# State-space stage: outputs on two column halves, lag products on four column quarters, preparation reordered

## What is computed

```python
h = rmsnorm(x, norm_mix[i])
a_bar = jnp.exp(lam * dt)
b_bar = ((a_bar - 1.0) / lam)[..., None] * lax.complex(b_re, b_im)
bu = jnp.einsum('blgh,gph->blgp', ug, b_bar)
_, states = lax.associative_scan(_ssm_combine, (a_seq, bu), axis=1)
y = jnp.einsum('blgp,ghp->blgh', states, c).real.reshape(bsz, length, D_MODEL)
y = jax.nn.gelu(y + d_skip * u)
val, gate = jnp.split(y @ w_glu, 2, axis=-1)
return val * jax.nn.sigmoid(gate)
```

## Time and profile before

| | us |
|---|---|
| median of 3 runs | 1874.41 (1874.4 to 1874.81) |
| the profiled execution, its own time | 1875.26 |
| its span, first to last instruction | 1873.5 |
| PE busy in the span | 1832.2 |
| end of the changed stage (first GLU product) | 144.8 |

### The profile page before, as it was taken

The page is one execution under the profiler, slowest core; times in us unless marked ns, Lnnn a source line. Parts: engine busy times, 40 slices in busy tenths (PEclk is TensorE's granted clock), DMA queues, the critical chain, the costliest instruction groups (busy, mean ns, idle before and its releaser), DMA issues.

```text
span 1873.5 us, 23935 instructions
## 1 busy us (share of the span) xinstructions
PE 1832.2 (98%) x9343; PEld 1476.4 (79%) x9343; DVE 1164.0 (62%) x1690; ACT 839.9 (45%) x1340; POOL 748.9 (40%) x429
## 2 busy tenths in 40 slices
PE   6999999999999999999999999999999999999998
PEld 5888888888887778668888888887776868888886
DVE  8974234735566588872356365641636658887978
ACT  6743343333335445683333233353457464343444
POOL 1214344343434368543443434334346454334322
PEclk9999999999999999999999999999999999999999
DMA  6424443052321222103532424125110223325041
GB/s 167 103 39 158 124 154 94 27 176 68 113 68 41 94 75 91 46 2 113 157 90 67 146 58 129 51 82 152 57 68 22 81 90 113 119 62 162 19 135 45
DMA packets 199979, 171.24 MB, mean 91 GB/s; under 512 B 19002, under 2 KB 174090, under 8 KB 199802
## 3 DMA queue, kind: packets, MB, share of 16 engines
q1 hardware_dynamic: 197554, 165.93, 29.5%
q10 hardware_dynamic: 2312, 3.78, 0.6%
HBM read 162.58 MB, written 2.65 MB: 88 GB/s over the span
## 4 chain that ended last, share of the span: by engine, by line
PE 88%; ACT 4%; DVE 4%; issue 1%; DMA 1%; POOL 1%; SPq 0%; POOLq 0%; DVEq 0%; ACTq 0%
PE PS L2644 75%; PE PS L3006 2%; PE PS L2997 2%; PE PS L3016 2%; DMA xp<-in_x 1%; PE PS L2542 1%; PE PS L2543 1%; PE PS L2563 1%; PE PS L2575 1%; DVE taken L2374 1%; PE PS L2956 1%; PE PS L2923 0%; ACT probs_t L1457 0%; PE PS L2584 0%; PE PS L2590 0%
## 5 line engine op out<-in xcount | busy, mean ns | idle before, releaser
L781 POOL TENSOR_TENSOR w_lo<-raw,w_hi 128x2048 fp32r<-128x2048 f32 x92 | 430.2, 4676 | 609.8 <-ACT w_hi L1074 608.4
L2644 PE MATMUL PS<-xT_hi,w_hi 128*128 128x512 f32 (+1 forms) x1160 | 444.4, 383 | 3.1 <-DVE xT_lo L1903 2.0
L2644 PE MATMUL PS<-xT_lo,w_hi 128*128 128x512 f32 (+1 forms) x1160 | 441.6, 381 | 0.0
L2644 PE MATMUL PS<-xT_hi,w_lo 128*128 128x512 f32 (+1 forms) x1160 | 441.4, 380 | 0.0
L1074 ACT ACTIVATE w_hi<-raw 128x2048 fp32r<-128x2048 f32 x105 | 201.2, 1916 | 332.0 <-PE PS L2644 332.0
L2644 PEld LDWEIGHTS PS<-xT_hi,w_hi 128*128 128x128 f32 x1160 | 217.8, 188 | 50.1 <-issue 8.6
L2644 PEld LDWEIGHTS PS<-xT_lo,w_hi 128*128 128x128 f32 x1160 | 217.8, 188 | 42.2
L2644 PEld LDWEIGHTS PS<-xT_hi,w_lo 128*128 128x128 f32 x1160 | 217.9, 188 | 41.1
L788 POOL TENSOR_TENSOR w_lo<-dn_raw,w_hi 128x1024 fp32r<-128x1024 f32 (+1 forms) x52 | 138.5, 2685 | 249.5 <-ACT w_hi L1225 249.5
L2644 PE MATMUL PS<-w_hi,xT_hi 128*128 128x512 f32 (+1 forms) x560 | 220.0, 393 | 1.0 <-issue 1.0
L2644 PE MATMUL PS<-w_hi,xT_lo 128*128 128x512 f32 (+1 forms) x560 | 216.6, 387 | 0.0
(11 more groups left out here) (425 smaller groups left out, 2843.2 us busy)
## 6 DMA issues: line engine op xcount, KB each, us to landing
raw<-in_ffn_w_gate_up SPq DMA_DIRECT2D x88, 512.0 KB, 5.1
dn_raw<-in_ffn_w_down SPq DMA_DIRECT2D x22, 1024.0 KB, 7.8
raw<-in_w_up SPq DMA_DIRECT2D x32, 512.0 KB, 5.4
dn_raw<-in_w_down SPq DMA_DIRECT2D x16, 1024.0 KB, 7.9
raw<-in_dsa_w_in SPq DMA_DIRECT2D x28, 512.0 KB, 4.4
raw<-in_w_in SPq DMA_DIRECT2D x21, 512.0 KB, 4.8
raw<-in_s_w_glu SPq DMA_DIRECT2D x16, 512.0 KB, 4.5
raw<-in_dsa_w_o SPq DMA_DIRECT2D x8, 512.0 KB, 4.5
```

What stands on the lines that cost most here:

```text
L781: pool.tensor_tensor(w_lo[:, g % 2, :], raw[:, r % 2, :], f32(w_hi[:, g % 2, :]), ALU.subtract).then_inc(w_split, 1)
L2644: ins = mm(o, a if weights_stay else c, c if weights_stay else a, start=first and n == 0, stop=last and n == 2, skip_group_check=onto)
```

## The change

1. **Outputs on two column halves.** `s5_out` is split. `s5_out_taps(b)` makes the eight taps products, `s5_out(b)` sixteen state products (the output map's two products, which DVE used to subtract, are now added by PE in PSUM). Groups 0 to 3 of a block go to PSUM rows 0 to 63 and groups 4 to 7 to rows 64 to 127, in turns. Gelu handles 128x512 instead of 64x1024, the `y` layout changes, and the turns on the way out are 32 transposes of 128x128. The GLU weights are loaded in the matching row order: four DMAs for a slot where there were two.
2. **Lags on four quarters.** The 8 groups go to PSUM rows 0, 32, 64 and 96, two each: 8 products of 16 columns, 16 of 112, and 4 for the skip term. `lag_out` becomes four instructions of 16x256. The lags have two PSUM banks in turns, so PE no longer waits for the last copy.
3. **Output map.** Two unlinked DVE products of 128x1024 (signs moved into the ACT copies of C), no difference.
4. **Preparation.** The powers take four linked instructions a step where there were six. ACT scales rows 0 and 4, makes table 0, then rows 1 to 3; DVE scales rows 5 to 7. PE turns five row sets ahead of the loop and three in its first pass; the second half of the value product and of `kv_done` moves behind the first `s5_in`.
5. **Tables.** Parts 1 to 3 are made by ACT in passes 0 to 2 of the block loop, behind the copies of the pass and ahead of its gelu; SP issues the copy of part b+1 behind the taps of block b.
6. **Order.** PE: rotate in, input, lags, turn of the input map, rotate out, output taps, output. ACT: lag copy first, then states.

```diff
@@ constants
-TURN_BANKS = [4, 5, 6, 0, 1, 2, 3, 7]
+U_BY_ACT, U_BY_DVE = (0, 4, 1, 2, 3), (5, 6, 7)
+TURN_BANKS, U_EARLY = [5, 1, 6, 2, 3, 0, 7, 6], 5
@@ SyncE
+                for b in range(2):
+                    for t in range(2):
+                        cols = slice(D * t + 256 * j, D * t + 256 * j + 256)
+                        put(raw_of(g) % 2, v[GP * b:GP * b + GP, :, t, :], glu[b][:, k:k + 4, cols])
...
                             for s in range(CH):
                                 sp.dma_start(tp[GH * s:GH * s + GH, :, s:CH, :].rearrange("p g t h -> p g (t h)"),
                                              lag[:, :, 0:CH - s, :].rearrange("p g t h -> p g (t h)")).then_inc(s5_taps, 16)
+                            if b < TABS - 1:
+                                table_copy(b + 1)
                             if b == 0:
-                                table_copy(1)
                                 sp.wait_ge(kv_sb, 2)
                                 sp.dma_start(kv_dram, kv_new[:, :, :]).then_inc(kv_out, 16)
-                                table_copy(2)
                             if b == 1:
-                                table_copy(3)
                                 glu_load(0, 0, 0)
@@ ScalarE
-            for s in range(CH):
+            for s in U_BY_ACT:
                 act.wait_ge(s5_rstd, 1 + s // (CH // 2))
-                if s == CH // 2:
-                    kv_copy(0)
                 act.activation(u[:, :, s, :], xp[:, s, :].rearrange("p (g h) -> p g h", h=GH), ACT.Copy,
                                scale=rstd[0:NC, s:s + 1]).then_inc(s5_u, 1)
+                if s == 4:
+                    act.wait_ge(s5_u, 2)
+                    table(0)
...
+                for q in range(4):
+                    ins = act.activation(lag[:, 2 * q:2 * q + 2, :, :].rearrange("p g t h -> p (g t h)"),
+                                         PS[32 * q:32 * q + GH, b % 2, 0:2 * P], ACT.Copy)
+                ins.then_inc(s5_lag_sb, 1)
...
             in_map_out(0)
+            kv_copy(0)
+            turned_rows(0, U_EARLY)
             lag_out(0)
-            table(0)
+            decay_out(0)
             kv_copy(1)
...
-            table(1)
-            table(2)
             for b in range(NB - 1):
+                lag_out(b + 1)
+                if b == 0:
+                    turned_rows(U_EARLY, NB)
                 states_out(b)
-                lag_out(b + 1)
                 decay_out(b + 1)
                 if b + 2 < NB:
                     in_map_out(b + 2)
-                if b == 0:
-                    table(3)
+                if b < TABS - 1:
+                    table(b + 1)
                 gelu(b)
@@ VectorE
-                link(tt(o[:, :, :, :], over_k(c_n, b, CH + 1), p_re, ALU.mult))
-                link(tt(tmp_a[:, :, :, :], over_k(c_s, b, CH + 1), p_im, ALU.mult))
-                tt(o[:, :, :, :], o[:, :, :, :], tmp_a[:, :, :, :], ALU.subtract).then_inc(s5_outa, 1)
+                tt(out_re[b % 3][:, :, :, :], over_k(c_n, b, CH), p_re, ALU.mult)
+                tt(out_im[b % 3][:, :, :, :], over_k(c_s, b, CH), p_im, ALU.mult).then_inc(s5_outa, 1)
...
+            dve.wait_ge(s5_rstd, 2)
+            for s in U_BY_DVE:
+                ts(u[:, :, s, :], xp[:, s, :].rearrange("p (g h) -> p g h", h=GH), rstd[0:NC, s:s + 1], None, ALU.mult).then_inc(s5_u_dve, 1)
...
-                    dve.wait_ge(x_hi_done, j0 + n_th + 1)
+                    dve.wait_ge(x_hi_done, j0 + n_th + (2 - n_th % 2 if view else 1))
@@ TensorE
+            def s5_out_taps(b):
+                pe.wait_ge(s5_taps, 16 * CH * (b + 1))
...
+                for g in range(GB // 2):
+                    for side in range(2):
+                        at = GB // 2 * side + g
+                        mm(s5_out_at(b, side, g), uT[:, GB * b + at, :], tp[:, at, :, :].rearrange("p t h -> p (t h)"), start=g == 0, stop=False)
...
+                for j in range(2):
+                    for q in range(4):
+                        g = GB * b + 2 * q + j
+                        mm(at(q, j)[:, 0:GH], b_n[:, g, :], c_n[:, g, :], start=j == 0, stop=False)
...
             for b in range(NB - 1):
                 s5_rotate_in(b)
                 s5_in(b + 1)
                 s5_lags(b + 1)
-                s5_rotate_out(b)
+                if b == 0:
+                    pe.wait_ge(s5_lag_sb, 1)
+                    pe.wait_ge(kv_sb, 2)
+                    u_turn(U_EARLY, NB)
                 if b + 2 < NB:
                     s5_in_turn(b + 2)
-                else:
+                s5_rotate_out(b)
+                if b == 0:
+                    pe.wait_ge(s5_ut_sb, NB)
+                s5_out_taps(b)
+                if b + 2 == NB:
                     s5_rotate_in(b + 1)
                 s5_out(b)
+            s5_out_taps(NB - 1)
             pe.wait_ge(s5_lag_sb, NB)
             s5_rotate_out(NB - 1)
-            s5_turn(0, 4)
+            s5_turn(0, 2)
             s5_out(NB - 1)
-            s5_turn(4, NB)
+            s5_turn(2, 4)
```

More of the change, by code:

```diff
@@ L256, in program @@
         small = place("small", "arena", 82 * KB, [P, 18, G])
[L257 to L260, removed]
+        pw = place("pw", "spare", 0, [P, 2, G, CH + 1])
+        pw_r, pw_i = pw[:, 0, :, :], pw[:, 1, :, :]
+        pw_is = place("pw_is", "spare", 4608, [P, G, CH + 1])
         uT = place("uT", "x_hi", 0, [P, G, NC])
@@ L1056, in states_out @@
                 act.activation(states[:, :, :].rearrange("p g c -> p (g c)"), PS[:, 5, :], ACT.Copy).then_inc(s5_x_sb, 1)
[L1058 to L1067, removed]
             def round_slot(g):
                 r = raw_of(g)
-                act.wait_ge(w_raw[r % 2], (r // 2 + 1) * 32)
+                act.wait_ge(w_raw[r % 2], 32 * (r // 2 + 1) + 32 * min(r // 2 + 1, GLU_SLOTS // 2))
                 if g >= 2:
@@ L1074, in round_slot, with turned_rows @@
                 act.activation(w_hi[:, g % 2, :], raw[:, r % 2, :], ACT.Copy).then_inc(w_rounded, 1)
+            def turned_rows(first, last):
+                for q in range(first, last):
+                    act.wait_ge(s5_ut, q + 1)
+                    act.activation(uT[:, GB * q:GB * q + GB, :].rearrange("p g c -> p (g c)"), PS[:, TURN_BANKS[q], :], ACT.Copy).then_inc(s5_ut_sb, 1)
             in_map_out(0)
+            kv_copy(0)
+            turned_rows(0, U_EARLY)
             lag_out(0)
-            table(0)
+            decay_out(0)
             kv_copy(1)
-            for q in range(8):
-                act.wait_ge(s5_ut, q + 1)
-                act.activation(uT[:, GB * q:GB * q + GB, :].rearrange("p g c -> p (g c)"), PS[:, TURN_BANKS[q], :], ACT.Copy).then_inc(s5_ut_sb, 1)
-            decay_out(0)
             in_map_out(1)
-            table(1)
-            table(2)
             for b in range(NB - 1):
+                lag_out(b + 1)
+                if b == 0:
+                    turned_rows(U_EARLY, NB)
                 states_out(b)
-                lag_out(b + 1)
                 decay_out(b + 1)
@@ L2522, in _, with kv_values @@
             ins.then_inc(kv_done, 1)
-            def kv_values(m):
-                for k in range(KT):
+            def kv_values(m, first=0, last=KT):
+                for k in range(first, last):
                     ins = mm(PS[:, 7, MEM * m:MEM * m + MEM], memT[:, k, P * m:P * m + P], w_kv[:, 1, k, :], start=k == 0, stop=k == KT - 1)
@@ L2532, in _, with s5_out_at @@
             kv_values(0)
+            def s5_out_at(b, side, g):
+                return PS[GP * side:GP * side + GP, 6 + b % 2, P * g:P * g + P]
+            def s5_out_taps(b):
+                pe.wait_ge(s5_taps, 16 * CH * (b + 1))
+                tp = taps[(b + 1) % 2]
+                if b >= 2:
+                    pe.wait_ge(s5_gelu, b - 1)
+                for g in range(GB // 2):
+                    for side in range(2):
+                        at = GB // 2 * side + g
+                        mm(s5_out_at(b, side, g), uT[:, GB * b + at, :], tp[:, at, :, :].rearrange("p t h -> p (t h)"), start=g == 0, stop=False)
             def s5_out(b):
                 pe.wait_ge(s5_x_sb, b + 1)
-                pe.wait_ge(s5_taps, 16 * CH * (b + 1))
-                tp = taps[(b + 1) % 2]
-                if b >= 1:
-                    pe.wait_ge(s5_gelu, b)
-                for g in range(GB):
-                    o = PS[0:NC, 6 + g // 4, P * (g % 4):P * (g % 4) + P]
-                    mm(o, uT[:, GB * b + g, :], tp[:, g, :, :].rearrange("p t h -> p (t h)"), start=True, stop=False)
-                    ins = mm(o, states[:, g, :], out_a[b % 3][:, g, 1:CH + 1, :].rearrange("p t h -> p (t h)"), start=False, stop=True)
+                for g in range(GB // 2):
+                    for m in (out_re, out_im):
+                        for side in range(2):
+                            at = GB // 2 * side + g
+                            ins = mm(s5_out_at(b, side, g), states[:, at, :], m[b % 3][:, at, :, :].rearrange("p t h -> p (t h)"),
```

(1 more changed line is left out.)

156 lines of the change are left out of this document (81 added, 75 removed).

## The result

The changed kernel took 1907.44 us (median of 4 runs, 1906.39 to 1909.1), the kernel before 1874.61 (1874.4 to 1875.08) beside it: ratio 1.0174, 95% interval 1.0162 to 1.0186, so 32.8 us slower. The forecast was 1895.9 with 1887 to 1904: the direction and the mechanism were right, the size was 11.5 us short and the time lies outside the range. The profiled execution had 1906.39 (span 1904.6), 31.1 us of span more than the one before.

The account below looks back on a forecast made before the run. PE was taken as the bound, 88% of the chain. Preparation, three table passes, quicker blocks and way out summed to +20.8 us at the GLU start; with 0.8 for low clock +21.5, forecast 1895.9 us, range 1887 to 1904.

Parts of the forecast that it names:

- a low clock behind the start: At the GLU's start: PE idle before it, so one 6.8 us low-clock stretch, half behind the start; 0.8 us at even odds.
- What PE and DVE gain: Block loop: overlapping column halves and quarters cut PE's block from 10.43 to 8.75 us and DVE's to 8.5.
- The ring: Block loop: table copies ahead of the next taps put tables into the lag-copy cycle; three passes 49.8 us, before 31.3.
- The passes: Passes 0, 1 and 2 of the block loop, lag copy to lag copy: 16.3, 18.0 and 15.5 us.
- The preparation: Ahead of the loop: PE's pause and 6.8 us of low clock; lag copy 1 at 69.6 instead of 67.94, +1.7 us.
- To rotate in of block 4: From lag copy 4 at 119.4 to block 4's rotate in at 124.3, where it was at 103.20: +21.1 us.
- The way out: From the end of block 7's lags to the first GLU product: 19.9 us instead of 16.0, +3.9.
- Blocks 4 to 7: End of the loop: two undisturbed blocks -3.4 us, first products of block 6 and lags of block 7 -0.8.
- The reload of the sine: ACT before a table in the loop: loading the sine table after gelu takes 1.28 us, without a further drain.
- The lighter ring: Rival: no clock fall in the preparation, no sine reload, quicker GLU issues and lag copy; +14, 1888 us; chance 0.14.
- the hidden ring: Rival: the table cycle stays hidden, so the loop gains 12 us less 9 to 12 elsewhere; 1873 us; chance 0.09.
- halves and quarters don't overlap: Rival, PE's outputs and lags: no overlap, blocks of 10.8 us on top of the waits; +31, 1905 us; chance 0.07.

Follow-up runs that it names:

- experiment 1: Changed kernel with only SP's order altered, the copy of table n issued behind the taps of block n, not ahead of them: 1880.9 us, ratio 1.0032.
- experiment 3: Kernel before with only the late tables: tables 1 to 3 made in passes 0 to 2, copied ahead of the next block's taps: 1893.3 us, ratio 1.0095.
- experiment 5: Changed kernel with a second lag buffer, SP's order untouched: 1892.15 us, ratio 1.0092.
- experiment 7: Kernel of experiment 1 with block 7's taps products moved behind the last rotate out and the first row turns: 1876.92 us, ratio 1.0011.
- experiment 8: Kernel of experiment 1 with the second value product whole ahead of the u turns and lag copy 0 ahead of row copies 3 and 4: 1878.1 us.
- experiment 9: Changed kernel with the edits of experiment 7 and experiment 8 and each table made one pass earlier: 1871.86 us, ratio 0.9985.
- Experiment 6: Changed kernel with the first GLU load (four issues) moved from behind the taps of block 1 to behind those of block 3: 1903.41 us, ratio 1.0151.
- The added products: Unused value products on PE before the u turns: twelve on experiment 9, 1868.52 us; on the changed kernel with the value product whole, twelve 1901.61, seven 1901.63.

## Why the prediction was right in kind and short in size

The sum was +20.8 at the GLU start; +30.8 was measured. The rest of the 11.5 us lies between profiled executions and medians: the execution before stood 0.85 us above its median, the changed one 1.05 below; and the 0.8 taken for a low clock behind the start came to 0.3. By the sum's own steps:

- **What PE and DVE gain: right.** Halves and quarters overlap. Block 8.49 us (8.75 forecast); outputs 1.02 + 1.75 = 2.77 (2.8); lags 0.21 + 0.78 + 0.06 = 1.05 (1.25, bounds 1.1 to 1.5, so just below them). The Trainium skill's 60 cycles for every matmul (TensorEngine Tiling (Array Packing), "Instruction Overhead") would make about 0.4 us, an estimate at 2.4 GHz, of the sixteen matmul instructions of 16 columns (eight products) if they stood in a row; the row has 0.21, so on the four quarters they overlapped at least in part. (The 0.19 for a round of 112 columns is a slip: 0.231 x 112/128 is 0.20; it changes nothing.)
- **The ring: right, and it is most of the loss.** Taps of blocks 1 to 3 were issued behind the table copies, at 82.48, 102.69 and 119.30, with only the key/value store and the GLU issues between. Experiments 1, 3 and 5 show it from three sides. Without it the kernel was still 6 us slower than before (experiment 1); experiments 7 to 9 win that back in the preparation, the way out and the place of the tables.
- **The passes: mis-sized, +4.5 us, the largest term of the miss and the step that failed.** 18.14, 19.75 and 16.45 against 16.3, 18.0 and 15.5. The links were the ones named; too small was SP's part. "I take 5.2 further on" cleared the 5.77 of the earlier trace rows of its slow issue as an accident, and the 1.2 for the table copies and 2.5 for the GLU issues were clean values too. A slow issue isn't an accident: an issue mostly takes 0.60, but every pass had at least one of about twice that or more, and in a closed ring it adds in full. The long issues and the landings in the chain:

```profile
80.58 1.23 SPq L594
...
83.16 1.72 SPq L607
...
88.13 1.84 DMA taps<-lag
...
119.92 1.14 SPq L607
...
124.33 1.84 DMA taps<-lag
```

With the 1.18 at 100.06 in pass 1 (shown above) the four long issues are 2.9 us over 0.60 each. By terms over the three passes: taps 6.25, 5.15 and 5.63 us (+1.4, and pass 1 as forecast), table copies +0.7, GLU issues 3.3 (+0.8), landings +1.0 (2.47 in pass 1 counted from the last issue's begin, where 1.8 was taken), ACT +0.5 (8.1 us from lag copy 2 to the end of its table, 7.9 forecast). Experiment 6 prices the GLU part.

- **The preparation: mis-sized, +2.3.** Lag copy 1 at 71.91 (69.6). The clock was low from 50.49 to 60.73, for 10.2 us and not 6.8; at half speed that is 1.7 of it. The row of the stretch (granted clock 0.50 behind the five engines):

```profile
50.50:60.70 10.20, 9.92 (x49) 8.62 (x49) 1.73 (x2) 3.29 (x6) 0.00 (x0) 0.50 0.07 15
```

- **To rotate in of block 4: +1.0.** Output 3 ran at the low clock: 3.68 us for products that take 1.75. I had put a priced term for the clock only in the preparation and behind the GLU's start, and here no more than "some low clock". PE stood idle for 6.4, 8.6 and 4.9 us ahead of outputs 1, 2 and 3, and the clock was low in each of these outputs; the last of them lay on the path.
- **The way out: mis-sized, +2.6.** 22.5 us from the end of lags 7 to the GLU start (19.9). The chain has the landing of the last taps at 2.76 (1.8 taken), and two pieces at the low clock: the rotate out 1.96 for 1.06, and the last turns 1.94 (the eight transposes just before them took 1.06 at full clock). Its rows:

```profile
159.21 2.76 DMA taps<-lag
...
162.01 1.09 PE PS L2552 x16
163.11 1.96 PE PS L2618 x2
...
169.54 4.08 DVE xT_lo L1880 x4
...
173.76 1.94 PE PS L2650 x8
```

- **Blocks 4 to 7: -0.5**, the quicker lags and outputs: 21.0 us from rotate in of block 4 to the end of lags 7, 21.5 by the sum. Together 2.3 + 4.5 + 1.0 + 2.6 - 0.5 = 9.9, which with 20.8 gives 30.7.
- **The reload of the sine: right.** 93.66 to 94.94, and the sine began at 94.95. The Trainium skill's drain of 1.38 us on top (ScalarE: Activation LUTs, "What ACT_TABLE_LOAD costs") isn't in this trace either; with it the two reloads would explain 2.8 of the miss, and they explain none of it.
- **The rivals.** The lighter ring and the hidden ring fell. That halves and quarters don't overlap fell by the rows above, although its time (1905) was the nearest.
- **The range** was too narrow upward. The mis-sized terms (issues, landing, clock) are missed upward when the clean value is taken, and its upper end stood 8 us above the middle. With the 5.77 of the earlier trace rows for each of the four taps on the path the sum is 4 x 0.57 = 2.3 higher, 1898 us; and an upper end that allowed for three more idle stretches at the 3.4 us which I gave the first would have stood at 1908 and held the time, though in part by luck: of the three, only the last lay on the path.

Not settled: what the clock's fall in the preparation costs by itself. The added products gave 3.3 us on one kernel and 2.1, within the noise, on the other, their number made no difference on the second, and the start of table 0, ahead of all this, already lay between 44.0 and 46.8 us from execution to execution. A way out without DVE's pair-wise wait wasn't tried.

## What to carry to other kernels

Ask of every instruction on an in-order queue not only what it waits for but what stands behind it; here two DMA issues ahead of eight others closed a ring that cost 26 us, and moving them behind gave that back. In a closed ring take the mean of the rows, long issues included, for these add up, and look for the link that is cheapest to cut (an order, a second buffer). And when a stage begins to wait, look at PE's clock too: it can be part of the price of the products that follow a wait on the path.

## What the runs showed of the hardware

- A DMA issue on SP mostly took 0.60 us, but eight in a row took 5.07 to 7.89 us over these runs; in the changed kernel's ring one in nine took 1.1 to 1.7.
- After waits of 3 to 9 us PE's granted clock often went to 0.5 (1.2 of 2.4 GHz), for 3.4 us in some places and for up to 13.7 in others. Over ten runs of one kernel (experiment 8) the mean clock moved from 0.992 to 0.996 and the time with it, from 1880.7 to 1874.2 us.
- Sixteen matmul instructions (eight products) of 16 columns on four array quarters took 0.21 us in the chain, thirty-two (sixteen products) of 112 columns 0.78.
